# Gather and scatter products of a mixture-of-experts loop: one float32 product in place of three bfloat16 parts

## The reference

```python
scores = sigmoid(x @ router)                    # 256 tokens x 64 experts
... # 4 of 8 groups, then the best 8 experts of each token, weights normalised, x 2.5
combine = sum(one_hot(eidx, 64) * wsel[..., None], axis=-2)
h = silu(einsum('btd,edf->btef', x, w_gate)) * einsum('btd,edf->btef', x, w_up)
routed = einsum('btef,efd->btd', h * combine[..., None], w_down)
shared = (silu(x @ ws_gate) * (x @ ws_up)) @ ws_down
return routed + shared
```

## Time and profile before

| | us |
|---|---|
| median of 3 runs (1361.14 to 1367.31) | 1364.74 |
| the profiled execution | 1364.09 |
| its span, first to last instruction | 1362.3 |
| PE busy, share of the span | 1291.1, 95% |
| DVE busy | 463.6, 34% |
| ACT busy | 345.2, 25% |
| mean HBM traffic | 372 GB/s |

### The profile page before, as it was taken

One profiled execution on the slowest core, in us unless ns is written; L12 is line 12 of the kernel. 1 busy time (PEld: TensorE's weight loads), 2 busy tenths in 40 slices (PEclk: granted clock), 3 DMA queues, 4 the chain that ended last, 5 costly groups with the idle time before them and its releaser, 6 DMA issues.

```text
span 1362.3 us, 24853 instructions
## 1 busy us (share of the span) xinstructions
PE 1291.1 (95%) x10054; PEld 679.5 (50%) x10054; DVE 463.6 (34%) x1188; ACT 345.2 (25%) x714; POOL 18.1 (1%) x23
## 2 busy tenths in 40 slices
PE   7989998999999998799989999899999999879997
PEld 5757646565444443444534554565545444334443
DVE  2556625323222222223231354532322322222223
ACT  2167033211212221122230244522221211112222
POOL 2100000000000000000000000000000000000000
PEclk9999999999999999899999999999999999999999
DMA  9796899999999999999999466889999999999995
GB/s 348 222 347 248 328 374 404 370 405 385 420 420 420 421 420 420 420 420 420 418 388 338 185 229 247 340 344 395 394 421 419 420 421 420 421 420 406 420 420 234
DMA packets 114515, 507.97 MB, mean 373 GB/s; under 512 B 19037, under 2 KB 27425, under 8 KB 64353
## 3 DMA queue, kind: packets, MB, share of 16 engines
q1 hardware_dynamic: 113136, 503.42, 92.3%
q0 software_dynamic: 1008, 2.45, 0.6%
q10 hardware_dynamic: 256, 0.49, 0.1%
HBM read 504.18 MB, written 2.14 MB: 372 GB/s over the span
## 4 chain that ended last, share of the span: by engine, by line
PE 84%; DMA 6%; DVE 5%; ACT 2%; issue 1%; SPq 1%; ACTq 0%; DVEq 0%
PE PS L883 82%; DMA ring<-in_moe_w_down 6%; DVE W L2263 1%; PE PS L1189 1%; DVE x L2138 0%; DMA rows<-in_norm_g 0%; DVE hT L2098 0%; PE PS L1520 0%; ACT W L1830 0%; ACT W L1829 0%; DVE W L2260 0%; PE PS L1278 0%; SPq L584 0%; SPq L573 0%; DVE W L2388 0%
## 5 line engine op out<-in xcount | busy, mean ns | idle before, releaser
L883 PE MATMUL PS<-ring,W 128*32 128x512 f32 (+5 forms) x3400 | 575.0, 535 | 7.2 <-DMA ring<-in_moe_w_down 5.9
L883 PE MATMUL PS<-W 128*128 128x128 bf16 (+7 forms) x3242 | 472.2, 353 | 5.7 <-DVE ring L2271 2.3
L883 PEld LDWEIGHTS PS<-ring,W 128*32 128x32 f32 (+2 forms) x3400 | 191.7, 120 | 214.1 <-issue 187.0
L883 PEld LDWEIGHTS PS<-W 128*128 128x128 bf16 (+4 forms) x3242 | 233.9, 111 | 120.6 <-issue 101.9
L883 PE MATMUL PS<-W,junk 128*128 128x128 bf16 x848 | 117.8, 221 | 10.4 <-issue 7.0
L2394 DVE TENSOR_TENSOR diag<-PS,diag 128x512 f32<-128x512 f32 x100 | 69.2, 692 | 151.0 <-ACT diag L1884 151.0
L2388 DVE COPY W<-PS 128x512 f32<-128x512 f32 x53 | 36.7, 692 | 239.6 <-PE PS L883 239.6
L883 PE MATMUL PS<-diag,W 128*128 128x512 bf16 (+2 forms) x424 | 112.9, 393 | 4.8 <-ACT diag L1886 2.2
L883 PE MATMUL PS<-ring,hT 128*128 128x512 f32 x256 | 115.1, 599 | 0.5 <-ACT hT L2029 0.3
L1884 ACT CAST diag<-PS 128x512 bf16<-128x512 f32 x100 | 58.5, 585 | 197.5 <-PE PS L883 197.5
L2371 DVE SCALAR_TENSOR_TENSOR W<-W,PS 128x256 f32<-128x256 f32 x52 | 25.0, 481 | 220.6 <-ACT W L1871 220.6
(11 more groups left out here) (285 smaller groups left out, 852.1 us busy)
## 6 DMA issues: line engine op xcount, KB each, us to landing
ring<-in_moe_w_down SPq DMA_DIRECT2D x104, 1024.0 KB, 17.9
ring<-in_moe_w_gate SPq DMA_DIRECT2D x88, 1024.0 KB, 16.9
ring<-in_moe_w_up SPq DMA_DIRECT2D x88, 1024.0 KB, 19.5
W<-in_moe_w_gate SPq DMA_DIRECT2D x40, 1024.0 KB, 15.6
W<-in_moe_w_up SPq DMA_DIRECT2D x40, 1024.0 KB, 18.3
W<-in_moe_w_down SPq DMA_DIRECT2D x25, 1024.0 KB, 16.6
ring<-in_mod_w SPq DMA_DIRECT2D x28, 768.0 KB, 9.1
ring<-in_mod_w SPq DMA_DIRECT2D x16, 1024.0 KB, 11.6
```

The costliest lines, as they stand in the source:

```text
L883: return eng.matmul(out, lhsT, rhs, start=first, stop=last, skip_group_check=True)
```

## The change

All three uses of the 0/1 matrix become one float32 product each, and every split into parts goes.

- `gather`: 8 x 2 = 16 float32 matmuls of 128 columns, from `xm` (the tokens in float32, two tiles of W), `S` in float32.
- `scatter`: 2 float32 matmuls of 512 columns per token half, from `out_rows` (float32); ACT copies its first half from PS and DVE its second, each after its own half of the down product.
- `turn_slots`: 2 float32 matmuls of 128 columns and 2 of 4; `com` holds the weights in float32, and `copy_slots` copies one column where it summed three.
- `rest_in_bank`, `weight_parts`, `rest_of_down`, `lowest_of_down`, `ident16` and `minus16` are gone. In layer 1 `turn_mods(7)` gets a wait on `scores_ready` of its own.
- The extra items change in the same way.

The core of the diff:

```diff
             def gather(sg_, j, Sb, ready=None):
...
-                        for part in range(3):
-                            for st in range(NS):
-                                ins = mm(PS[:, 6 + half, i * P:(i + 1) * P],
-                                         parts[part][:, st * D + k * P:st * D + (k + 1) * P], Sb[:, st, :],
-                                         part + st == 0, part + st == 3)
+                        for st in range(NS):
+                            ins = mm(PS[:, 6 + half, i * P:(i + 1) * P],
+                                     xm[st][:, k * P:(k + 1) * P], Sb[:, st, :], st == 0, st == NS - 1)
...
             def turn_slots(sg_, item, j, buf):
...
-                    mm(PS[:, 7, 256 + st * P:256 + (st + 1) * P], S[buf][:, st, :], ident16, st == 0, True)
-                    ins = mm(PS[:, 7, 0:12], S[buf][:, st, :],
-                             com3[:, st, bass.ds(item, 4), :].rearrange("p e q -> p (e q)"), False, st == 1)
+                    mm(PS[:, 7, 256 + st * P:256 + (st + 1) * P], S[buf][:, st, :], ident, st == 0, True)
+                    ins = mm(PS[:, 7, 0:4], S[buf][:, st, :], com[:, st, bass.ds(item, 4)], False, st == 1)
...
             def scatter(sg_, j, st, buf, first=False):
...
-                for part in range(3):
-                    eng.wait_ge((sg_.o_act, sg_.o_act, sg_.o_dve)[part], 3 * j + (2, 3, 3)[part])
-                    for half in range(2):
-                        mm(PS[:, 2 * st + half, :], wT[buf][:, st * P:(st + 1) * P],
-                           oparts[part][:, half * 512:(half + 1) * 512], first and part == 0, False)
+                for half in range(2):
+                    eng.wait_ge((sg_.o_act, sg_.o_dve)[half], j + 1)
+                    mm(PS[:, 2 * st + half, :], wT[buf][:, st * P:(st + 1) * P],
+                       out_rows[:, half * 512:(half + 1) * 512], first, False)
...
             def copy_down(sg_, j):      # ACT
-                for half in range(2):
-                    eng.wait_ge(sg_.down_done, 2 * j + half + 1)
-                    eng.copy(oparts[0][:, half * 512:(half + 1) * 512], PS[:, 4 + half, :]).then_inc(sg_.o_act, 1)
-                eng.wait_ge(sg_.o_dve, 3 * j + 2)
-                eng.copy(oparts[1], orest).then_inc(sg_.o_act, 1)
+                eng.wait_ge(sg_.down_done, 2 * j + 1)
+                eng.copy(out_rows[:, 0:512], PS[:, 4, :]).then_inc(sg_.o_act, 1)
...
                 def group(it, last, first=False, drained=False):      # DVE
...
-                            rest_of_down(s, j)
-                            copy_slots(s, j + 1, wT32 if last else wT[(i + 1) % 2])
-                            lowest_of_down(s, j)
+                        copy_down(s, j)
+                        if not ((last or drained) and i == 1):
+                            copy_slots(s, j + 1, wT[(i + 1) % 2])
```

More of the change, by code:

```diff
@@ L296, in trunk @@
         c = Carve()
-        parts = [junk[:, :].bitcast(BF16), c(D).bitcast(BF16), c(D).bitcast(BF16)]
+        xm = [c(D) for _ in range(NS)]
         xg, hE, hT2 = c(KD, P), c(F), c(2, P)
[L301 to L304, removed]
+        S = [c(NS, P) for _ in range(2)]
+        wT = [c(NS * P) for _ in range(2)]
         wslot = c(8)
-        posL, com3 = c(ITEMS, NS), c(3 * ITEMS * NS // 2).bitcast(BF16).rearrange("p (s e q) -> p s e q", s=NS, q=3)
-        com_rest = c(NS, COLS)
+        posL, com = c(ITEMS, NS), c(NS, ITEMS)
+        c(ITEMS * NS // 2 + NS * COLS)
         x_down_w = W[:, c.at:c.at + F * D // P]
@@ L536, in gain_rows, with xm_rows @@
             return gains[16 * n:16 * n + 16, :].rearrange("(s k) p -> s (k p)", s=NS).partition_broadcast(P)
-        def part_rows(part, b):
+        def xm_rows(b):
             st, half = divmod(b, 2)
-            return parts[part][:, st * D:(st + 1) * D].rearrange("p (k q) -> p k q", k=KD)[:, :, half * 64:(half + 1) * 64]
+            return xm[st].rearrange("p (k q) -> p k q", k=KD)[:, :, half * 64:(half + 1) * 64]
         def bank_rows(b):
@@ L1304, in moe @@
                     turn_plain(b)
-                for b in range(4):
-                    rest_in_bank(0, b)
                 if L:
+                    eng.wait_ge(s.scores_ready, L + 1)
                     turn_mods(7)
-                for b in range(4):
-                    rest_in_bank(1, b)
                 eng.wait_ge(s.mask_ready, L + 1)
@@ L1482, in moe @@
                     one_pass(p)
[L1483 removed]
+                scatter_whole(s, (L + 1) * PASSES - 1, 1)
             moe(0)
@@ L1906, in moe @@
                     eng.wait_ge(s.xm_turned, 4 * L + b + 1)
[L1907 to L1911, removed]
+                    eng.copy(xm_rows(b), bank_rows(b)).then_inc(s.xm_act, 1)
                 act.settle()
@@ L2388, in copy_gathered, with copy_down @@
                 eng.tensor_copy(xg[:, 4:8, :].rearrange("p k n -> p (k n)"), PS[:, 7, :]).then_inc(sg_.xg_dve, 1)
-            def rest_of_down(sg_, j):
-                for half in range(2):
-                    cols = slice(half * 512, (half + 1) * 512)
-                    eng.wait_ge(sg_.o_act, 3 * j + half + 1)
-                    eng.tensor_tensor(orest[:, cols], PS[:, 4 + half, :], oparts[0][:, cols], ALU.subtract)\
-                       .then_inc(sg_.o_dve, 1)
-            def lowest_of_down(sg_, j):
-                eng.wait_ge(sg_.o_act, 3 * j + 3)
-                eng.tensor_tensor(oparts[2], orest, oparts[1], ALU.subtract).then_inc(sg_.o_dve, 1)
-            def copy_half_down(sg_, j):
+            def copy_down(sg_, j):
                 eng.wait_ge(sg_.down_done, 2 * j + 2)
-                eng.tensor_copy(orest[:, 512:1024], PS[:, 5, :]).then_inc(sg_.o_dve, 3)
+                eng.tensor_copy(out_rows[:, 512:1024], PS[:, 5, :]).then_inc(sg_.o_dve, 1)
             def route(L):
@@ L2481, in paired @@
                 def paired(first, end):
-                    return lambda q: com3[:, :, first:end, q].rearrange("p s (e two) -> p s e two", two=2)
+                    return com[:, :, first:end].rearrange("p s (e two) -> p s e two", two=2)
                 eng.wait_ge(s.ranks_done, L + 1)
@@ L2497, in moe @@
                    .then_inc(s.plan_dve, 1)
-                weight_parts(paired(0, 2 * STATIC), bc(comb[:, :, 0:STATIC], 3, 2),
-                             com_rest[:, :, 0:2 * STATIC].rearrange("p s (e two) -> p s e two", two=2))\
-                    .then_inc(s.pos_ready, 1)
+                eng.tensor_copy(paired(0, 2 * STATIC), bc(comb[:, :, 0:STATIC], 3, 2)).then_inc(s.pos_ready, 1)
                 if L:
```

79 lines of the change are left out of this document (24 added, 55 removed).

## The result

| | before | after |
|---|---|---|
| median, us | 1364.16 (4 runs) | 1479.96 (4 runs, 1478.58 to 1483.33) |
| profiled execution, us | 1364.09 | 1480.22 |
| span, us | 1362.3 | 1478.4 |

The ratio is 1.085, with a 95% interval from 1.082 to 1.088. The profiled executions differ by 116.1 us; 107 were forecast.

A forecast was written before the change was run, and what follows sets the result against it. PE was taken to bound the kernel, with DMA close behind. Gather +45, scatter +42 and slots +34 made +121 us, less 9.0 and 5.2, so +107 and 1471 us; 1446 to 1503 us held 8 in 10.

The forecast's parts named there:

- The bound: Expert loops: PE sets the pace and DMA follows closely; added PE time is lost at once, gains beyond 9.0 us to DMA.
- 149.8 us against 131.7: DMA's time for a round's 20 experts against PE's for its eight passes; DMA some 18 us behind in a round.
- the 9.0 us: PE's waits on weights in both layers, which go once DMA no longer falls behind: -9.0 us.
- The gather: Float32 gather at 0.110 us a record: +0.85 us, 53 times, +45 us; bounds +32 to +49.
- The rival on weight loads: Float32 loads of 0.191 us set the pitch of gather and slots: +281 us, 1645 us; chance 0.04.
- The scatter: One token half in float32 takes 1.72 us instead of 1.30: +0.42 us, 100 times, +42 us.
- The slots: `turn_slots` in float32: +0.65 us, 53 times, +34 us; least certain term, +13 to +70 us.
- a sign of being wrong: Small products of the slots standing further apart than 0.12 us would show the forecast wrong.
- those 5.2 us: Behind pass 17, PE's waits for ACT and DVE to make parts go, 2.6 us in each layer: -5.2 us.
- the start of the layers: Eight `rest_in_bank` matmuls and ACT copies go beside DVE's routing: counted as nothing, at most a microsecond or so back.
- DMA swallowing the change: Stream at 420 GB/s is the true pace and the extra 121 us run in slack: 1359 us, no change; chance 0.03.
- A float32 record at a bfloat16 record's price: Record counts decide, at 0.0556 and 0.217 us a record: -80 us of PE, but 1355 us through DMA; chance 0.02.

The follow-up runs named there:

- two_parts_both: Kernel before with the third bfloat16 part left out of the gather and of the scatter; 1349.17 us, ratio 0.991.
- drained32: Kernel before with the scatter of pass 17 alone as one float32 product, fed by copies of halves; 1361.53 us against 1363.51.
- scatter32_only: Kernel before with the scatter alone as one float32 product, gather and slots still in bfloat16 parts; 1395.22 us against 1364.64.
- slots16: Changed kernel with turn_slots alone back in bfloat16 and combine weights rounded to bfloat16; 1444.91 us against 1479.96.
- half_down_before: Kernel before with half of each down matrix left out of its load, the loaded half used twice; 1349.41 us, ratio 0.989.
- warm: Changed kernel with 8 unread float32 products keeping PE busy while it waits for the routing; 1475.79 us, ratio 1.083.
- two_parts: Kernel before with the third bfloat16 part left out of the gather; 1351.10 us, ratio 0.990.
- two_parts_half_down: Kernel before with the gather's third part and half of each down matrix's load both left out; 1301.93 us, ratio 0.956.
- half_down_after: Changed kernel with half of each down matrix left out of its load, the loaded half used twice; 1476.09 us.

## Why the prediction was right, point by point

**The bound.** Right, and shown from both sides. A cut in PE's work is worth 13.5 us of 47 because DMA is close behind; a cut in DMA's is worth 15 because PE is ahead; together PE's 47 us count in full. Full DMA windows in the earlier trace rows would have misled, while PE's empty list of waits did not. And the asymmetry that the forecast drew from 149.8 us against 131.7 held: added PE time is lost at once, but for the waits that it removes.

One number of that argument was off. Not every pass lasts 16.46 us: four of the first eighteen have shared-expert products on top and last 20 to 23 us. From pass 1 to pass 17 of layer 0 PE took 286.5 us in the kernel before, 143.3 for eight passes, and takes 326.7 now, 163.4. (The times are those of `turn_hidden`, 246.48 to 532.98 and 252.32 to 579.06 us.) So in these two rounds DMA was 6.5 us behind in a round and not 18, and it is now 14 us ahead and not level: 149.8/163.4 of 420 GB/s is 385, and the window has 380. Only in the last round, at 16.43 us a pass, does the forecast's 131.7 hold. The conclusion on the 9.0 us stands, with more room than was claimed.

**The gather.** +0.89 us where +0.85 was forecast; the pitch is 3.56/32 = 0.111 us, between the 0.110 taken and the 0.1125 of the earlier trace rows. The rival on weight loads is out for the stream: the 31 loads under this gather last longer than its pitch, and are hidden. The Trainium skill, "TensorE: Matmul & The Clock Gate", section "Weight-path perf modes — Fast Weight Load (FWL) and DoubleRow", excludes float32 from the fast load; the traces agree that the load is slower, 0.191 us against 0.099 for the bfloat16 gather's loads, and disagree with drawing the price of a stream from it.

**The scatter: the term that was too small.** The second half costs 1.72 us as worked out. The first half costs 1.82. It follows the gate and up products, which run in column tiles; PEld's timeline of the changed kernel shows full-width float32 loads that begin together with the first records of the group:

```profile
657.42 0.30 PEld L878 LDWEIGHTS PS<-diag,W 128*128 128x128 f32 x2 [0.84 <-issue]
657.96 0.19 PEld L878 LDWEIGHTS PS<-diag,W 128*128 128x128 f32 x1 [0.24 <-issue]
...
668.41 0.30 PEld L878 LDWEIGHTS PS<-con,W 128*128 128x128 f32 x2 [0.84 <-issue]
```

Inside a group each load starts a record ahead; the first one starts with its own matmul, and the first record takes 0.10 us longer than the others. The slots, behind the tiled down product, show the same (0.33 us for their first two records, 0.31 for the same two of the second token half). The bfloat16 group in the same place takes 1.30 us for either half, so next to nothing of its 0.1 us load is seen. That it is the longer float32 load which shows where the tiling changes is a reading of these rows; no run here tried it. I had the change of tiling at 0.1 us in both kernels. Priced as measured, the three terms are 53 x 0.89 + 50 x 0.94 + 53 x 0.69 = 130.7 us in place of 121: 5 us more for the scatter, 2.6 for the slots and 2.2 for the gather. This is where most of the missing 9 us is.

**The slots.** +0.69 us (+0.65 forecast), between bounds that reached from +0.24 to +1.33. The nearest row was the right one for the sum but not for the parts: in the pass above two 4-column records take 0.14 us and the two 128-column records behind them 0.31, which together is again 0.11 a record. In PEld's timeline the loads of these records, in groups of two, begin 0.22 us apart, whatever the columns:

```profile
668.63 0.30 PEld L878 LDWEIGHTS PS<-W 128*128 128x128 f32 x2
668.85 0.30 PEld L878 LDWEIGHTS PS<-con,W 128*128 128x128 f32 x2
669.08 0.30 PEld L878 LDWEIGHTS PS<-W 128*128 128x128 f32 x2
```

A load lasts 0.19 us here, but the next one begins 0.11 us after its start. So the price of a 4-column record, here and in the 0.1025 us of the earlier trace rows, reads as the distance between the starts of the weight loads. The forecast had named as a sign of being wrong that the small products of the slots stand further apart than 0.12 us. Taken alone the 128-column ones do, by 0.16 us on average; all eight together don't, (0.99 - 0.1)/8 = 0.111.

**What comes back.** The 9.0 us of waits on weights went, all of them, and went with the scatter's 0.94 us alone. Behind pass 17 PE goes from the down product to the scatter with no wait; those 5.2 us went too. I had counted nothing for the start of the layers, and there the sign was other than thought: the first gathers took 5.4 and 6.5 us instead of 3.7, +4.5 us in sum, because work that looked like overhead had kept PE busy.

**What the sum left out.** 130.7 - 14.2 + 4.5 = +121.0, against +116.1 measured. Behind the scatter of pass 17 of layer 0, ahead of the next gather, PE of the kernel before has this gap (PE's timeline, 545 to 558 us). PE of the changed kernel has a shorter one, ahead of the last 4 of the gather's 32 records:

```profile
551.65 0.39 PE L883 MATMUL PS<-W,junk 128*128 128x128 bf16 x2 [5.28 <-issue]
```

```profile
592.67 0.60 PE L878 MATMUL PS<-W 128*128 128x128 f32 x4 [1.15 <-issue]
```

"Issue" is time in which PE waited for nothing that the profile shows. The kernel before has a second such gap of 1.75 us behind the extra item of layer 1, ahead of the last 5 of that gather's 48 records, which the changed kernel lacks. That is 5.9 us less. The gather behind the gap of 5.28 us also ran at a granted clock of 0.50 and took 4.6 us instead of 2.7, 2 us that the changed kernel doesn't lose there; it loses 3 us in layer 1's extra item, whose products ran in part at the lower clock, and the kernel before 1.2 us in the gate and up products behind its own. With these the sum is 121.0 - 5.9 - 2 + 3 - 1.2 = +115, within 2 us of the measured number, and stretches at the lower clock move from execution to execution by as much. The forecast had neither the +4.5 nor the -5.9; that they nearly cancel is luck.

What sets the gap was not tried by a run. In the other traces the longest is 4.7 us (`two_parts_both`), 4.4 (`drained32`), 4.3 (`scatter32_only`, with a second one of 1.9), 4.2 (`slots16`), 4.1 (`half_down_before`), 2.8 (`warm`), 2.1 (`two_parts`), 1.9 (`two_parts_half_down`) and 1.1 (`half_down_after`). A lighter load of DMA changes it by 0.0 to 1.2 us (1.15 against 1.14, 2.12 against 1.91, 5.28 against 4.07). The DMA view has one thing in common. In each of these gaps, or just ahead of it, queue q8, which the page calls "instruction", moves a packet of 16 KB, and PE goes on 1.2 to 1.5 us after the packet's end. For the gap above the packet lasts from 549.14 to 550.24 us (DMA view, 549.1 to 550.3 us):

```profile
q8 instruction: 1, 0.02, 5.7%
```

So the gap looks like PE waiting for the next piece of its program, behind the run-time loop over the extra items. This is a reading; why the packet comes in time in one kernel and late in another stays open.

**The rivals.** Weight loads setting the pitch would have given 1645 us; the gather's pitch of 0.111 us excludes it. In the gather the columns and the starts of the loads come to the same 0.11 us, so which of the two sets its pitch these runs can't tell. DMA swallowing the change is excluded by 30.6 us for the scatter alone. A float32 record at a bfloat16 record's price would have needed under 0.083 us for 128 columns.

## What to carry to other kernels

When PE and DMA are both full, ask who waits for whom, and how much work each has in a round: here DMA kept up with PE by nothing but the six experts loaded ahead, so PE's losses counted in full, less the 9 us of waits that they removed, and its gains beyond some 13 us not at all. An exact product of a float32 operand with a 0/1 matrix is cheaper here as three bfloat16 parts than as one float32 product (1.30 against 1.72 us for a token half's scatter), as long as ACT and DVE have time to make the parts under other work; where nothing covers them, as behind pass 17, no difference could be measured. In this kernel the next gain is in bytes or in the balance, not in PE's count: two parts in the gather give 13.5 us, at the price of the lowest of the tokens' three bfloat16 parts, and two parts in the scatter as well give nothing further.

## What the runs showed of the hardware that I had not expected

- A full-width float32 weight load that follows column-tiled products shows with 0.10 us on the first record. Within a stream a 0.19 us load is hidden at a pitch of 0.111 us (31 loads in 3.54 us).
- Among products of 4 and 128 columns the loads begin 0.11 us apart whatever the columns, so that two 4-column float32 records and two 128-column ones behind them take 0.45 us, as four of 128 columns would.
- Taking eight products away from a stretch in which PE waits for DVE brought a granted clock of 0.53 to 0.64 for the gather behind it, 5.4 and 6.5 us instead of 3.7. With products put back it was 1.00 and 3.7 us.
- The two cuts: PE's 47 us were worth 13.5 us at the full traffic and 47.5 us at five sixths of the experts' bytes. Of the 33.5 us lost, 25.5 were waits on weights; part of the rest was the lower clock that came with them (0.980 instead of 0.990 over the span).
- In or just ahead of each of the gaps of 1.1 to 5.3 us behind pass 17 for which the profile shows no cause, a 16 KB packet of the instruction queue ends 1.2 to 1.5 us before PE goes on.
